# Seven products in place of eight for x, B and C of the in-projection

## What is computed

```python
# per layer: u = rms_norm(h), then u @ w_in, columns split into
#   q | six K/V parts | gates | z | x B C | dt
SPLIT_SIZES = (D_ATT, KV_DIM, KV_DIM, KV_DIM, KV_DIM, KV_DIM, KV_DIM, ATT_HEADS * 3, D_SSM, D_CONV, SSM_HEADS)

def mamba2_mixer(z, xBC, dt_raw, conv_w, conv_b, ...):
    xBC = lax.conv_general_dilated(xBC, conv_w[:, None, :], ...)   # causal, depthwise, 4 taps
    xBC = jax.nn.silu(xBC + conv_b)
    xs = xBC[..., :D_SSM] ...; Bm = ...; Cm = ...
```

## Time and profile before

| | |
|---|---|
| median of 3 runs | 1191.0 us (1188.29 to 1193.54) |
| the profiled execution, its own time | 1193.55 us |
| its span, first to last instruction | 1191.8 us |
| mean granted TensorE clock | 0.977 of full |
| PE busy | 94% of the span |
| DVE, ACT, POOL busy | 57%, 26%, 10% |

### The profile page before, as it was taken

How to read it: one execution, slowest core, us unless ns; L and a number is a source line. 1 busy time by engine, 2 the same in 40 slices (tenths; PEclk the granted TensorE clock), 3 DMA queues, 4 the chain that set the end, 5 groups by cost and what they waited for, 6 DMA issues and landing times. The chain is left out here.

```text
span 1191.8 us, 14782 instructions
## 1 busy us (share of the span) xinstructions
PE 1120.5 (94%) x4905; PEld 673.8 (57%) x4906; DVE 675.9 (57%) x1531; ACT 306.0 (26%) x734; POOL 119.7 (10%) x173
## 2 busy tenths in 40 slices
PE   6999999999999999999999988999984999999995
PEld 3544664444566777777777778555552444444442
DVE  2422223332344666677666459644459887887883
ACT  2311121111233434343333356322211000000000
POOL 0000000000000000000000043000002233333332
PEclk9999999999999999999999989999996999999998
DMA  6210330200000000000000070332244988899432
GB/s 239 68 40 0 115 114 1 70 1 17 1 2 3 4 2 4 2 2 2 2 1 1 1 283 1 98 145 106 106 154 149 329 271 294 313 380 353 165 102 80
DMA packets 72066, 119.79 MB, mean 101 GB/s; under 512 B 14305, under 2 KB 49217, under 8 KB 72009
## 3 DMA queue, kind: packets, MB, share of 16 engines
q1 hardware_dynamic: 60920, 88.08, 21.5%
q0 software_dynamic: 11088, 30.95, 7.4%
HBM read 105.90 MB, written 21.50 MB: 107 GB/s over the span
## 5 line engine op out<-in xcount | busy, mean ns | idle before, releaser
L1441 DVE STREAM_TRANSPOSE big_w<-big_w 32x256 f32<-32x256 f32 x400 | 174.3, 436 | 32.1 <-DMA big_w<-hn_dram,misc 25.6
L1609 PE MATMUL ps<-ring_gate_up,big_w 128*128 (+1 forms) x400 | 182.0, 598 | 2.0 <-DVE big_w L1441 2.0
L462 PE MATMUL ps<-big_w,big_u 128*128 128x512 f32 (+1 forms) x448 | 174.4, 544 | 0.0
L1043 ACT ACTIVATE big_u<-ps,big_w 128x384 f32<-128x384 f32 (+15 forms) x192 | 90.0, 522 | 187.6 <-DVE big_w L1104 169.4
L983 PE MATMUL ps<-ring_down,big_u 128*128 128x65 f32 x912 | 115.7, 276 | 16.7 <-DVE big_u L1119 8.6
L983 PEld LDWEIGHTS ps<-ring_down,big_u 128*128 128x128 f32 x912 | 109.5, 192 | 36.4 <-ACT big_u L1052 14.7
L462 PEld LDWEIGHTS ps<-big_w,big_u 128*128 128x128 f32 x448 | 83.9, 192 | 75.9 <-issue 69.9
L1609 PEld LDWEIGHTS ps<-ring_gate_up,big_w 128*128 128x128 f32 x400 | 74.8, 192 | 87.6 <-issue 87.6
L952 PE MATMUL ps<-ring_down,misc 97*128 97x512 f32 (+3 forms) x320 | 122.9, 494 | 1.3 <-ACT ring_gate_up L1062 1.3
L1865 PE MATMUL ps<-big_w,big_u 128*128 128x512 f32 x256 | 114.7, 595 | 0.9 <-ACT big_u L2007 0.9
L1104 DVE TENSOR_REDUCE big_w<-ps 128x2 f32<-128x768 f32 (+15 forms) x96 | 78.2, 815 | 62.1 <-PE ps L957 53.3
(11 more groups left out here) (323 smaller groups left out, 1161.1 us busy)
## 6 DMA issues: line engine op xcount, KB each, us to landing
ring_gate_up<-in_w_gate SPq DMA_DIRECT2D x16, 1024.0 KB
ring_gate_up<-in_w_up SPq DMA_DIRECT2D x16, 1024.0 KB
ring_down<-in_w_down SPq DMA_DIRECT2D x16, 1024.0 KB
big_w<-in_w_in SPq DMA_DIRECT2D x10, 1024.0 KB, 7.2
misc<-in_x SPq DMA_DIRECT2D x16, 512.0 KB, 3.4
big_w<-in_w_out SPq DMA_DIRECT2D x8, 512.0 KB, 6.4
hn_dram<-big_u SPq DMA_DIRECT2D x8, 512.0 KB, 2.7
out<-ring_gate_up SPq DMA_DIRECT2D x8, 512.0 KB, 3.6
```

The source lines that it names most:

```text
L462: last = nc.tensor.matmul(ps[:, b, 0:width], uT[:, k, c * P:(c + 1) * P], wbuf[:, n % 2, k, 0:width], start=(k == 0), stop=(k == KD - 1))
L1043: last = nc.scalar.activation(weights(j)[:, i * n:(i + 1) * n], src, ACT.Exp, bias=neg[:, br, h:h + 1])
L1441: last = nc.vector.transpose(dst[j * 32:(j + 1) * 32, :, i * 32:(i + 1) * 32], src[i * 32:(i + 1) * 32, :, j * 32:(j + 1) * 32])
L1609: last = nc.tensor.matmul(ps[:, 2 + b, :], xT[:, b, k, :], ring_gu[:, bass.ds(at + k * 2 * D_EXP, BANK)], start=(k == 0), stop=(k == KD - 1))
```

## The change

x, B and C are computed in four pairs of channel tiles. For one pair, the weights are four quarters (two channel tiles by two halves of the input columns), and the activations `uT` are four quarters (two halves of the input columns by two halves of the tokens). A product of a weight quarter with an activation quarter is four matmuls. The plain way takes eight such products for a pair. The new code takes seven, by Winograd's form of Strassen's method: some products take a sum or difference of quarters as weights, and some take one as activations.

The sums of weights (S1 to S4, 128x512 each, four for each pair) and those of activations (T1 to T4, 128x2048 each, once) are made on POOL by `tensor_tensor`. T1 and T2 lie in the upper half of `big_w`, T3 and T4 where `z` will be, S1 and S2 in `xn1` or in an unused part of `o_att`, S3 and S4 in place of the weight quarters that are no longer needed. The outputs are put together in part by going on adding in a PSUM bank that ACT has copied in the meantime, and in part by twelve additions on DVE (`x_add`, 128x512, one operand in PSUM and one in SBUF). ACT still makes sixteen copies.

The loads of X0 and X1 (two of 1 MB each) become eight of 512 KB. The first pair goes to `conv[:, 2:4]` ahead of KVB on the SP queue, pairs 1 and 2 are issued when the K/V products are through, pair 3 when pair 1 is. z's chunk is issued when the fourth product of the last pair is through; before, it was issued when X0 was through.

The diff, cut:

```diff
+    N_PAIR, N_PROD = KD // 2, 7
+    w_of_pair = [[conv[:, 2 + i, 3:3 + D] for i in range(2)]] + \
+        [[M["big_w"][:, (2 * b + i) * D:(2 * b + i + 1) * D] for i in range(2)] for b in (0, 1, 0)]
+    T1, T2 = halves(M["big_w"][:, KD * BANK:])
+    T3, T4 = halves(z[:, :, :].rearrange("p c n -> p (c n)"))
+    x_banks = lambda p: [(4, 5, 6), (5, 6, 4), (6, 4, 5)][p % 3]
+    z_bank = lambda c: (7, 5, 6, 4)[c]
...
@@ sync @@
+                if n == Z_:
+                    sp.wait_ge(x_full, N_PROD * (N_PAIR - 1) + 4)
...
+            load_x_weights(0)
             load_w(KVB)
-            load_w(X0)
...
-            load_w(X1)
+            sp.wait_ge(m_full, 3 * NT)
+            load_x_weights(1)
+            load_x_weights(2)
+            sp.wait_ge(x_full, 2 * N_PROD)
+            load_x_weights(3)
             load_w(Z_)
-            sp.wait_ge(m_full, NT * Z_)
+            sp.wait_ge(x_full, N_PAIR * N_PROD)
...
@@ tensor @@
+            def product_channels(p, n):
+                a, b, c = x_banks(p)
+                a11, a12, _, a22 = w_quarters(p)
+                s1, s2, s3, s4 = w_sums(p)
+                bank, left, right, starts = [(a, a11, B11, True), (b, a12, B21, True), (a, s2, T2, False), (c, s1, T1, True),
+                                             (a, s3, T3, False), (c, s4, B22, False), (a, a22, T4, False)][n]
+                if n == 0:
+                    pe.wait_ge(s_wx[p], 32)
+                if p == 0 and n in (0, 1, 3):
+                    pe.wait_ge(kn_ready, 2 * NT - 3 + (0, 1, None, 2)[n])
+                elif n == 0:
+                    pe.wait_ge(x_added, 3 * (p - 1) + 1)
+                elif n == 1:
+                    pe.wait_ge(x_added, 3 * p)
+                elif n in (2, 4, 5):
+                    pe.wait_ge(x_copied, 4 * p + {2: 1, 4: 2, 5: 3}[n])
+                elif n == 3:
+                    pe.wait_ge(x_copied, 4 * p)
+                else:
+                    pe.wait_ge(x_added, 3 * p + 2)
+                if n >= 2:
+                    pe.wait_ge(x_sums, 4 * p + [2, 1, 3, 4, 1][n - 2])
+                    if p == 0:
+                        pe.wait_ge(u_sums, [3, 2, 1, 1, 4][n - 2])
+                for k in range(4):
+                    last = nc.tensor.matmul(ps[:, bank, :], left[:, k, :], right[:, k, :], start=(k == 0 and starts),
+                                            stop=(k == 3), skip_group_check=True)
+                last.then_inc(x_full, 1)
...
@@ scalar @@
+            for p in range(N_PAIR):
+                a, b, s = x_banks(p)
+                lo, hi = 2 * p, 2 * p + 1
+                x_copy(p, 0, lo, 0, a)
+                if p >= 1:
+                    silu(lo - 2)
+                    silu(hi - 2)
+                x_copy(p, 2, lo, 1, a)
...
+                x_copy(p, 3, hi, 1, s)
+                x_copy(p, 6, hi, 0, a)
+            silu(KD - 2)
             silu(KD - 1)
...
@@ gpsimd @@
+            def sums_of_weights(p):
...
+                if p == 1:
+                    pool.wait_ge(t_free, T_X + 2 * NT)
+                elif p >= 2:
+                    pool.wait_ge(x_full, N_PROD * (p - 2) + 4)
+                pool.wait_ge(s_wx[p], 32)
+                nc.gpsimd.tensor_tensor(s1, a21, a22, add).then_inc(x_sums, 1)
+                pool.wait_ge(x_sums, 4 * p + 1)
+                nc.gpsimd.tensor_tensor(s2, s1, a11, sub).then_inc(x_sums, 1)
+                nc.gpsimd.tensor_tensor(s3, a11, a21, sub).then_inc(x_sums, 1)
+            def last_sum(p):
...
+                pool.wait_ge(x_full, N_PROD * p + 2)
+                pool.wait_ge(x_sums, 4 * p + 3)
+                nc.gpsimd.tensor_tensor(s4, a12, s2, sub).then_inc(x_sums, 1)
+            pool.wait_ge(t_free, T_X)
+            o.mark(nc.gpsimd.tensor_tensor(T3, B22, B12, sub))
+            sums_of_weights(0)
+            pool.wait_ge(m_full, 2 * NT)
+            o.done(nc.gpsimd.tensor_tensor(T1, B12, B11, sub))
+            o.done(nc.gpsimd.tensor_tensor(T2, B22, T1, sub))
+            o.mark(nc.gpsimd.tensor_tensor(T4, B21, T2, sub))
+            for p in range(N_PAIR):
+                last_sum(p)
+                if p + 1 < N_PAIR:
+                    sums_of_weights(p + 1)
...
@@ vector @@
             for m in range(KD):
-                dve.wait_ge(m_free_act, 2 * m + 2)
+                p, (a, b, s) = m // 2, x_banks(m // 2)
+                if m % 2 == 0:
+                    x_add(p, 1, m, 0, b, 1)
+                    x_add(p, 4, m + 1, 1, a, 3)
+                    x_add(p, 5, m, 1, s, 2)
+                    dve.wait_ge(x_added, 3 * p + 3)
+                else:
+                    dve.wait_ge(x_copied, 4 * p + 4)
```

## The result

The changed kernel takes 1177.07 us (median of 6 runs, 1173.83 to 1179.86), the kernel before 1191.93 us in 6 runs beside it. The ratio is 0.9882 with a 95% interval of 0.986 to 0.9904, a gain of 11 to 17 us. The prediction was 1177.3 us.

What follows compares the result with a forecast made beforehand. It took x, B and C to be bound by PE's number of matmuls. Four products fewer, at 3.43 us each, give -13.73 us with nothing back: 1191.0 - 13.7 = 1177.3 us, range 1174.7 to 1183.

Steps and rivals of the forecast that it cites:

- PE bounds the stretch, and a record is worth 0.429 us: x, B and C: limited by matmul count; four products of 3.43 us fewer save 13.73 us.
- The seams cost nothing: PE, x, B and C: 28 groups instead of 16, with their waits, add no time.
- Copies, additions, the chain: ACT and DVE per pair: all hidden; odd convolution ends 7.0 us into the next pair, SiLUs about 8.1.
- The sums on POOL: Sums of weights and activations: 5.7 us per T, 1.4 per S, none late for PE.
- z's weights: End of x, B and C: landing 7.2 us after their event, near 263 us, 3 us before PE needs them.
- POOL beside DVE: Shared SBUF access: up to 0.82 us lost per DVE instruction, but POOL works where DVE is idle; nothing taken.
- Rival 1: DVE's convolution held whole by POOL's four sums, ACT's copy late: PE loses 19.5 us, 1196.8 us; chance 4%.
- the room: DVE's chain into the next pair: 4.8 us of delay fit before product 4 would wait for ACT's copy.
- The clock: PE in x, B and C: stays at 2.4 GHz; a fall there would prove the prediction wrong.
- rival 3: z's weights or T2 late: PE stalls 0.5 to 4.1 us, a clock fall adding as much; 1178 to 1186; chance 4%.
- The median: Whole kernel: 1191.0 us less 13.7 gives 1177.3 us.

Runs made afterwards that it cites:

- eighth: Changed kernel with an eighth product of four matmuls added back per pair, all else kept: 1189.82 us, ratio 0.9989 to the kernel before.
- uncovered: Changed kernel with product 2 directly behind product 0 in each pair: x, B and C stretch 100.01 us, 3.65 longer.
- port3idle: Changed kernel with three unread 1024-column POOL additions in pairs 0 to 2, straight behind the sums while DVE waits: stretch 96.36 us.
- port: Changed kernel with five unread 1024-column POOL additions in pairs 0 to 2, beside DVE's convolutions: 1199.53 us, stretch 122.48 us.
- port3conv: Changed kernel with three unread 1024-column POOL additions in pairs 0 to 2, beside DVE's convolutions: stretch 110.77 us.
- zlate5: Changed kernel with z's weights issued one product later, behind the last pair's fifth product: stretch 97.51 us, 1.15 longer.
- zlate7: Changed kernel with z's weights issued only behind the last pair's last product: PE waits 8.8 us, `attend` begins at 316.50 against 304.78.

## Why the prediction was right, point by point

- *PE bounds the stretch, and a record is worth 0.429 us.* Right. 13.73 us forecast, 96.36 against 110.09 measured, and "eighth" gives it back to 0.01 us.
- *The seams cost nothing.* Right: 28 groups without a gap. "uncovered" shows what a copy costs without cover, 0.9 us; I had said 0.8.
- *Copies, additions, the chain.* Right to 0.1 us, at 7.0 and 8.1 us into the pair.
- *The sums on POOL.* Right in effect; the size taken from the scaling was too long (5.7 for 4.5, 1.4 for 1.27), on the safe side. T2 was wanted at 176.74 by the prediction's own terms and not at 176.9; with tens of us to spare nothing hangs on it.
- *z's weights.* Right in effect, but the term was too short: 8.0 us for 7.2. I took the end of DMA traffic for the moment at which PE can begin. Room 2.3 us and not 3.
- *POOL beside DVE.* Right for one of the two reasons given. The first, that POOL works where DVE is idle, holds (port3idle). The second, that a collision costs at most 0.82 us, is false: 2.0 us beside an addition of 1024 columns, 0.9 beside one of 512. The rows showed three single DVE instructions of 512 columns beside a POOL instruction that reads one tensor; here DVE's are of 1024 columns and POOL reads two, and no run tells which of these makes the difference. Rival 1's path from a late DVE to a late PE was right. In pair 1 of "port" the odd convolution ends 18.9 us into the pair and product 4 starts at 20.6; the rival had 18.5 and 20.2. That the delay came out alike is chance, for it was made by five additions that the changed kernel does not have. The rival's own cause was four sums of 2.9 us each; they take 1.27, and beside DVE they cost it 3.6 us together, under the room of 5.1. So by these rows a pair's four sums alone would not have stopped PE even beside the convolution; this is an estimate. What the rival left out is the clock behind each pause: 19.5 us priced, 26.1 in "port".
- *The clock.* In the stretch full, as said. For rival 3 I had let a fall cost as much as the pause of 4.1 us; measured, it was 2.2 to 2.9 us behind each of six pauses of 3.6 to 8.8 us, and did not grow with their length.
- *The median.* 1177.07 against 1177.3. That closeness is luck in part. The two medians differ by 14.9 us and not 13.7, since the kernel before came out at 1191.93 in its six runs and not at 1191.0. The interval of the ratio is 5 us wide, and executions differ by 4.7 us in `attend` alone.

What stays open: a run in which POOL's own sums, and nothing more, lie beside DVE's convolution was not made; by port3conv's rows PE should not notice it. Why the granted clock of `attend` differs between executions is open too.

## What to carry to other kernels

Where PE streams without a gap, count matmuls: one removed is worth its spacing to the last digit, if each thing added has a product's time beside it, and that can be checked before by writing the clock of one period with the ends of every copy, sum and load in it. When work is given to GpSimd, look at what VectorE does in the same microseconds and not at how busy GpSimd is: the same three additions cost nothing in one place and all of a 14 us gain in the other. If VectorE has the room, it makes such sums in half the time and cannot collide with itself.

## What the runs showed of the hardware that I had not expected

- A GpSimd `tensor_tensor` of 1024 columns (2.4 us alone, 3.0 here) cost a VectorE instruction with two SBUF inputs 2.0 us, one of 512 columns (1.27 alone, up to 2.24 here) 0.9 us; a memset cost it nothing.
- The fall of the clock behind a PE pause is not small beside the pause. Pauses of 3.63, 3.65, 4.92, 6.67 and 6.72 us were followed by eight records in 6.34, 6.40, 5.79, 5.94 and 6.38 us in place of 3.60, and one of 8.79 us by sixteen in 9.92 in place of 7.03: 2.2 to 2.9 us each time. Behind pauses of 2.0, 1.0 and 0.7 us in the x, B and C stretch and ahead of z it stayed at 2.4 GHz.
- A short pause is not always safe. The barrier ahead of `attend` stops PE for 0.86 us in all 13 executions; in the 5 us behind it the granted clock was 1.00 in eleven of them and 0.66 in two, zlate5 and zlate7. Why in these is not shown.
- `attend` took 363.8 to 370.2 us in executions of the same instructions, with the granted clock of single stretches at 0.90 to 1.00, though PE's waits for ACT and DVE were the same (7.7 and 8.6 us at the largest line of each). A gain of half a per cent can't be read from two single executions of this kernel; the length of the changed stretch repeats to 0.02 us.
